# Gated linear attention: level products over the later half-blocks alone, two token tiles to a PSUM bank

## What is computed

```
bcum = jnp.cumsum(gi, axis=2)                                  # log decays, per key channel
diff = bcum[:, :, :, None, :] - bcum[:, :, None, :, :]
decay = jnp.exp(jnp.where(causal, diff, NEG_INF))
attn = jnp.einsum('bhid,bhjd,bhijd->bhij', qi, ki, decay)      # i the query, j the key, j <= i
o_intra = jnp.einsum('bhij,bhje->bhie', attn, vi)
```

## Time and profile before

| | |
|---|---|
| median of 3 runs | 1090.76 us (1087.79 to 1096.67) |
| the profiled execution's own time | 1091.74 us |
| its span, from first to last instruction | 1089.9 us |
| TensorE busy | 1007.9 us, 92% |
| TensorE weight loads busy (beside the products) | 831.4 us, 76% |
| VectorE busy | 446.7 us, 41% |
| ScalarE busy | 442.5 us, 41% |
| GpSimd busy | 191.7 us, 18% |
| mean granted TensorE clock | 0.961 of full speed |

### The profile page before, as it was taken

How to read it: one execution, slowest core, us unless ns; L and a number is a source line. 1 busy time by engine, 2 the same in 40 slices (tenths; PEclk the granted TensorE clock), 3 DMA queues, 4 the chain that set the end, 5 groups by cost and what they waited for, 6 DMA issues and landing times.

```text
span 1089.9 us, 13989 instructions
## 1 busy us (share of the span) xinstructions
PE 1007.9 (92%) x5164; PEld 831.4 (76%) x5164; DVE 446.7 (41%) x826; ACT 442.5 (41%) x757; POOL 191.7 (18%) x176
## 2 busy tenths in 40 slices
PE   1899998999898999999989999399999999899994
PEld 1687766888787878878878888388888888788883
DVE  2214534343214555555666652822323232323335
ACT  1642233242334565656774433523333333322222
POOL 1232222332341333323440000100000000000001
PEclk9999997997999999999999999599999999999998
DMA  5421111341223222226428532022222222212221
GB/s 185 137 77 58 59 39 58 93 156 62 71 86 100 92 93 68 92 97 230 138 78 299 192 119 101 23 75 98 97 97 95 97 96 96 96 62 98 95 72 78
DMA packets 37492, 110.58 MB, mean 101 GB/s; under 512 B 4065, under 2 KB 8161, under 8 KB 36930
## 3 DMA queue, kind: packets, MB, share of 16 engines
q1 hardware_dynamic: 37200, 109.44, 29.8%
q10 hardware_dynamic: 242, 0.47, 0.1%
HBM read 94.16 MB, written 12.58 MB: 98 GB/s over the span
## 4 chain that ended last, share of the span: by engine, by line
PE 88%; DVE 4%; ACT 3%; DMA 2%; issue 2%; POOL 1%; POOLq 0%; DVEq 0%; ACTq 0%
PE bank L1395 25%; PE bank L1396 24%; PE bank L1397 24%; PE bank L1455 3%; PE bank L559 2%; DMA onehot<-distance_onehot 2%; PE bank L551 1%; PE bank L573 1%; PE bank L550 1%; PE bank L571 1%; PE bank L517 1%; PE bank L577 1%; ACT w_hi L786 1%; ACT band L806 1%; DVE x L1281 0%
## 5 line engine op out<-in xcount | busy, mean ns | idle before, releaser
L1395 PE MATMUL bank<-h_hi,w_lo 128*128 128x512 f32 (+1 forms) x712 | 286.4, 402 | 4.8 <-DVE cqs L1126 3.0
L1396 PE MATMUL bank<-h_lo,w_hi 128*128 128x512 f32 (+1 forms) x712 | 281.6, 395 | 0.0
L1397 PE MATMUL bank<-h_hi,w_hi 128*128 128x512 f32 (+1 forms) x712 | 281.0, 395 | 0.0
L786 ACT ACTIVATE w_hi<-w_raw 128x1024 fp32r<-128x1024 f32 (+1 forms) x87 | 91.3, 1051 | 215.2 <-PE bank L1397 214.9
L1395 PEld LDWEIGHTS bank<-h_hi,w_lo 128*128 128x128 f32 (+1 forms) x712 | 136.2, 191 | 39.1 <-issue 12.6
L1397 PEld LDWEIGHTS bank<-h_hi,w_hi 128*128 128x128 f32 (+1 forms) x712 | 135.7, 191 | 29.9
L1396 PEld LDWEIGHTS bank<-h_lo,w_hi 128*128 128x128 f32 (+1 forms) x712 | 136.2, 191 | 26.1
L719 POOL TENSOR_TENSOR w_lo<-w_raw,w_hi 128x1024 fp32r<-128x1024 f32 (+1 forms) x37 | 86.9, 2349 | 209.9 <-ACT w_hi L786 209.9
L972 ACT ACTIVATE w_hi<-w_raw 128x1024 fp32r<-128x1024 f32 x44 | 46.7, 1061 | 157.2 <-PE bank L1397 157.2
L1328 DVE TENSOR_TENSOR w_lo<-w_raw,w_hi 128x1024 fp32r<-128x1024 f32 x44 | 54.0, 1226 | 104.1 <-ACT w_hi L972 104.1
L726 POOL TENSOR_TENSOR sc<-sc,ast 128x512 f32<-128x512 f32 (+1 forms) x96 | 66.2, 721 | 143.8 <-DVE ast L490 109.9
(11 more groups left out here) (257 smaller groups left out, 1531.7 us busy)
## 6 DMA issues: line engine op xcount, KB each, us to landing
w_raw<-wpack SPq DMA_DIRECT2D x147, 512.0 KB, 3.3
gate_logits<-gl_out SPq DMA_DIRECT2D x24, 256.0 KB, 2.2
gl_in<-gate_logits SPq DMA_DIRECT2D x24, 256.0 KB, 3.6
xs<-x_in SPq DMA_DIRECT2D x4, 512.0 KB, 9.3
bias_bands<-band SPq DMA_DIRECT2D x1, 2048.0 KB, 8.3
fullb<-bias_bands SPq DMA_DIRECT2D x16, 128.0 KB, 2.6
ckx<-cks SPq DMA_DIRECT2D x16, 128.0 KB, 2.5
ob<-gla_out SPq DMA_DIRECT2D x2, 1024.0 KB, 6.1
```

What stands on the lines that cost most here:

```text
L786: sa.activation(wh[:, b, 0:n], raw[:, s, 0:n], ACT.Copy).then_inc(w_hi, 1)
L1395: mm(out, ll, rh, start=start, stop=False, skip_group_check=True)
L1396: mm(out, lh, rl, start=False, stop=False, skip_group_check=True)
L1397: return mm(out, lh, rh, start=False, stop=stop, skip_group_check=True)
```

## The change

The seven levels with a half-block get two bank steps in place of four: for each head only the 64 tokens of later halves are streamed, so a head's product is 128 by 64 and two tiles with four heads each fill a bank. The order of the 16 matmuls in a bank step is by array row half, with one `other_rows` in each. VectorE copies a pair of tiles with one `copy_predicated` whose destination and mask are strided to the later halves. The diagonal keeps its form, under new functions `level_own` and `gla_pick_own`. The list `AUX` and the waits that name a level's last tile follow.

```diff
-AUX = (["gates", "z0", "z1", "bT0", "bT1"] + [f"lv{l}_{t}" for l in range(8) for t in range(NT)]
+AUX = (["gates", "z0", "z1", "bT0", "bT1"] + [f"lv{l}_{t}" for l in range(7) for t in range(2)] + [f"lv7_{t}" for t in range(NT)]
...
-                    aux_full(sa, "lv5_3")
+                    aux_full(sa, "lv5_1")
...
-                    aux_full(ve, f"lv{l - 2}_3")
+                    aux_full(ve, f"lv{l - 2}_1")
...
-                for t in range(NT):
+                s = LEVELS[l]
+                for t in range(2):
                     aux_full(ve, f"lv{l}_{t}")
...
                     if l > 0:
                         aux_out(ve, f"lv{l - 1}_{t}")
-                    ve.copy_predicated(attnT[:, t, :, :], lmask[:, l:l + 1, :].broadcast_to([P, 4, P]),
-                                       aux_bank(f"lv{l}_{t}")[:, :].rearrange("p (h c) -> p h c", h=4)
+                    later = attnT[:, 2 * t:2 * t + 2, :, :].rearrange("p t h (n u s) -> p (t h) n u s", u=2, s=s)
+                    below = lmask[:, l, :].rearrange("p (n u s) -> p n u s", u=2, s=s)
+                    ve.copy_predicated(later[:, :, :, 1, :],
+                                       below[:, :, 1, :].unsqueeze(1).broadcast_to([P, 8, 64 // s, s]),
+                                       aux_bank(f"lv{l}_{t}")[:, :].rearrange("p (h n s) -> p h n s", h=8, s=s)
                                        ).then_inc(aux_free[AUX_AT[f"lv{l}_{t}"] % 2], 1)
+            def gla_pick_own():
+                for t in range(NT):
+                    aux_full(ve, f"lv7_{t}")
+                    aux_out(ve, f"lv6_{t // 2}")
+                    ve.copy_predicated(attnT[:, t, :, :], lmask[:, 7:8, :].broadcast_to([P, 4, P]),
+                                       aux_bank(f"lv7_{t}")[:, :].rearrange("p (h c) -> p h c", h=4)
+                                       ).then_inc(aux_free[AUX_AT[f"lv7_{t}"] % 2], 1)
...
             def level(l):
+                s = LEVELS[l]
+                for pair in range(2):
+                    name = f"lv{l}_{pair}"
+                    aux_free_for(name)
+                    te.wait_ge(z_ready, 2 * l + 2)
+                    for odd in range(2):
+                        if odd:
+                            other_rows(last)
+                        for t in range(2):
+                            for p in range(2):
+                                both = zz[64 * odd:64 * odd + 64, l % 2, 512 * p + P * (2 * pair + t):512 * p + P * (2 * pair + t) + P]
+                                at_ = 256 * t + 64 * (2 * p + odd)
+                                last = mm(aux_bank(name)[:, at_:at_ + 64], both,
+                                          both.rearrange("p (n u s) -> p n u s", u=2, s=s)[:, :, 1, :], start=True, stop=True)
+                    last.then_inc(aux_done, 1)
+            def level_own():
                 for t in range(NT):
-                    name = f"lv{l}_{t}"
+                    name = f"lv7_{t}"
...
-                if 6 <= c < 14:
+                if 6 <= c < 13:
                     level(c - 6)
+                if c == 13:
+                    level_own()
```

More of the change, by code:

```diff
@@ L1163, in _ @@
                                      b3[:, :, P - 1:P].broadcast_to([P, 8, P]), b3, ALU.subtract).then_inc(e_ready, 1)
-                    gla_pick(7)
+                    gla_pick_own()
                     ve.wait_ge(ex_ready, 10)
@@ L1442, in level @@
             def level(l):
+                s = LEVELS[l]
[14 more added lines that the diff above has]
+            def level_own():
                 for t in range(NT):
-                    name = f"lv{l}_{t}"
+                    name = f"lv7_{t}"
                     aux_free_for(name)
-                    if l < 7:
-                        te.wait_ge(z_ready, 2 * l + 2)
                     for h in (0, 2, 1, 3):
@@ L1452, in level @@
                         cols = slice(512 * p + P * t, 512 * p + P * t + P)
-                        kk = zz[b:b + 64, l % 2, cols] if l < 7 else gk[b:b + 64, cols]
-                        qq = zz[b:b + 64, l % 2, cols] if l < 7 else gq[b:b + 64, cols]
-                        last = mm(aux_bank(name)[:, P * h:P * h + P], kk, qq, start=True, stop=True)
+                        last = mm(aux_bank(name)[:, P * h:P * h + P], gk[b:b + 64, cols], gq[b:b + 64, cols],
+                                  start=True, stop=True)
                     last.then_inc(aux_done, 1)
```

## The result

The changed kernel takes 1101.29 us (median of 20 runs, 1095.86 to 1108.30), the kernel before 1091.28 (20 runs, 1087.63 to 1096.67). The ratio is 1.0096, with a 95% interval of 1.0076 to 1.0116. The forecast was 1083 us, with a range of 1077 to 1091. The profiled executions are 11.6 us apart in span (1101.5 against 1089.9).

A forecast was written before the change was run, and what follows sets the result against it. TensorE, busy 92% of the span, was taken to bound the kernel. Level stages shrink from 4.57 to 3.44 us, saving 6.8 to 7.9 us in seven; from the 1090.76 median this gave 1083 us, range 1077 to 1091.

The forecast's parts named there:

- granted clock 1.00 in all seven: Sign of the forecast case: TensorE's clock stays at full speed through all seven edited level stages; that case had 67%.
- rival A: Clock falls in the thinner level stages, 3.4 us lost per fall; a fall in each of seven gives 1107 us; 12%.
- Moving columns halved: Level products: record spacing follows the weight columns, staying 0.11 us, so halved streaming buys nothing between records.
- Rival C: Level products: record spacing follows the moving columns after all, saving 2.26 us a level, 15.8 us: 1075 us; 7%.
- The tail: At two row waits and the hand-over to the projection: shorter last record (218 ns, not 272) saves 0.054 us each.
- steps one and three: First and last eight one-sided loads of a level stage: 1.21 and 1.08 us before taking off the shorter tail.
- Step two: Middle of a level stage, eight odd beside eight even loads: halves overlap, added loads 0.059 us each, 1.31 us.
- Rival B: Middle step: the second pair does not overlap the first, a stage takes 4.3 us, saving only 2 us: 1089; 12%.
- Waits: In a level stage: four row waits become two and the one bank wait goes, as two banks hold the level.
- VectorE's copies: 14 of 28 copies go, 11 us beside TensorE, worth nothing directly; strided copy taken at 0.79 us, bound at twice that.
- rival D: The strided copy is so dear, 2.6 us against 0.79, that VectorE binds: a little over 1091 us; 2%.
- What else must be ready: Weight split, ScalarE's `gv` copies and exponential, and DMA issues are in time, so the shorter stages meet no new wait.

The follow-up runs named there:

- run 2: Changed kernel with its order kept, but each product streams all 128 columns again (scores not the reference's): 1087.94 us, ratio 0.9955.
- run 3: Changed kernel with the 64 moving columns taken contiguous, as the first 64 tokens, in place of the strided later ones: 1100.69 us, ratio 1.0067.
- run 8: Changed kernel with 96 moving columns on average (odd heads 128, even 64) and the two row halves by turns in the middle step: 1082.96 us, ratio 0.9923.
- run 6: Kernel before, all 128 columns and four tiles, each level cut into five pieces inside the next projection chunk: 1092.12 us, ratio 1.0018.
- run 7: Changed kernel with odd heads first and streaming 128 columns, even heads 64, so 96 on average: 1094.75 us, ratio 1.0033.
- run 10: Repeat of run 8 (changed kernel with 96 columns on average and row halves by turns): 1085.73 us, ratio 0.9940.
- run 1: Kernel before with only the moving columns halved to 64 and copies narrowed likewise, old order kept: 1101.71 us, ratio 1.0095.
- run 9: Changed kernel with 64 moving columns, its only edit being row halves by turns in the middle of a level: 1092.89 us, ratio 1.0007.
- run 4: Changed kernel with each level's products cut at the row waits into three pieces inside the next projection chunk: 1089.49 us, ratio 0.9975.
- run 5: Run 4's kernel with the middle piece's two row halves issued by turns, one odd, one even: 1086.30 us, ratio 0.9959.

## Why the prediction was wrong

**The step that failed** is "granted clock 1.00 in all seven": rival A was given 12% and decided all. What the prediction held against it was that the `w1k` chunk, with 66 columns to 0.057 us, kept the clock at 1.00 for 3.64 us. I took its share of streaming time, about half, as the same thing. It did not carry over. The chunk uses 128 rows in one stretch of 3.6 us, the level stages 64 rows in seven stretches; which difference counts stays open, since no run varied it. The clock had also fallen behind the neighbouring `w1v` chunk, so one stretch that holds was weak evidence for seven that repeat. The row that should have weighed more is the earlier trace rows: a stream bound by its weight loads, in which the columns do not fill the interval, fell within 3 us of its start with no idle time in it. The price of a fall was set at 3.4 us, that of a fall of 6.8 us; only four of the seven were so long, and the mean price is 2.5. The chances of this rival do not fit together either: three falls or more got 6%, and the six or more that a loss of over 1% needs got 7%.

The Trainium skill, in "TensorE: Matmul & The Clock Gate", section "Why this matters for your kernels", warns of idle gaps between bursts of matmuls. No such gap explains these falls: the longest idle time of a stage's load engine was 0.35 us, in the stages at which the clock fell and in those of before alike. What differs between run 2, with no fall, and the changed kernel, with seven, is the columns streamed at the same number of loads.

**Moving columns halved: spacing.** Right. One-sided loads are (0.96 - 0.19) / 7 = 0.11 us apart with 64 columns as with 128. Rival C is out.

**The tail.** Right in size: the load engine idles 0.20 us at a row wait in place of 0.25, and steps one and three measure as forecast. The record itself does not show it: its median is 272 ns after as before, not the 218 that the prediction took; only the waits got shorter. Weight loads of a stage at full clock after, answering to the earlier trace rows:

```profile
101.69 0.96 PEld L1469 LDWEIGHTS bank<-zz 64*128 64x128 f32 x8 [0.35 <-issue]
102.85 1.46 PEld L1469 LDWEIGHTS bank<-zz 64*128 64x128 f32 x16 [0.20 <-PE bank L1469]
104.51 0.96 PEld L1469 LDWEIGHTS bank<-zz 64*128 64x128 f32 x8 [0.20 <-PE bank L1469]
105.55 0.29 PEld L1408 LDWEIGHTS bank<-w_hi,h_lo 128*128 128x128 f32 x1
```

Step one 102.85 - 101.69 = 1.16 (forecast 1.21 - 0.05), step three 1.04 (1.08 - 0.05).

**Step two was mis-sized:** 104.51 - 102.85 = 1.66 us against 1.31 - 0.05 = 1.26. The added eight loads were priced at 0.059 each, as if the halves overlapped all along; they overlap only from the sixth load on. Rival B is true in part: 0.4 of its 0.8 us. With turns the step is 114.02 - 112.82 = 1.20, and the stage 3.40, the 3.44 of the forecast. Had the clock held, the change as written would have saved 7 x 0.71 = 5.0 us and not 7.9, about 1086 us: the forecast of 1083 would have missed by 3.

**Waits.** The bank wait is gone and four row waits are two, as said.

**VectorE's copies.** Right for five levels of seven: the strided copy takes 0.70 to 0.74 us there, against the 0.79 taken. At half-blocks 2 and 1 all four copies take 1.31 us, inside the bound of twice 0.79 but not foreseen: the products of the earlier trace rows showed no such step. Runs 2 and 3, which leave the copies alone, have the same step (1.31 to 1.32 us). TensorE never waits for them, so it costs nothing here, and rival D (2.6 us a copy) is out. Line 1090, all seven levels, duration ns as in the earlier trace rows, then copies of half-blocks 4 and 2:

```profile
L1090 DVE COPY_PREDICATED attnT<-lmask,bank x14: 701/732/1315, 91.3 to 164.9; 128x512 f32<-128x512 uint16 x14
```

```profile
138.84 0.71 DVE L1090 COPY_PREDICATED attnT<-lmask,bank 128x512 f32<-128x512 uint16 x1 [6.36 <-PE bank L1469]
...
151.53 1.31 DVE L1090 COPY_PREDICATED attnT<-lmask,bank 128x512 f32<-128x512 uint16 x1 [7.27 <-PE bank L1469]
```

**What else must be ready.** Right: TensorE is busy throughout every chunk behind a stage.

## What to carry to other kernels

Before thinning a stretch of matmuls, ask what sets their interval. If it is the weight load, fewer moving columns buy little time (0.21 us of 4.07 a stage here), and the granted clock may fall, as it did at every stage here; what follows is unedited dense work at half speed, the dearest place to lose. It can be worth streaming columns that nobody reads (run 8). Where products use half of the rows, issue the two halves by turns.

## What the runs showed of the hardware

- Falls of the granted clock from 1.00 to 0.50 in or right behind the seven level stages, in one profiled execution of each kernel: with 128 columns a record, none (before, run 2; in run 6 one, behind 1.8 us of idle time); with 96, four (run 7), and none or one where the halves go by turns (runs 8, 10); with 64, six or seven (after, runs 1, 3, 9), with or without stride, turns or the old order; with 64 between dense products, none (runs 4, 5).
- TensorE lets the two row halves run side by side, but with eight records of one in front it started the other only after five (run 7). By turns, 16 loads take 0.97 us (run 9) and not 1.46.
- A change between 64-row and 128-row products costs a little more than the row wait that it can cover: 9.71 us interleaved against 9.54 (run 4).
- A `copy_predicated` of 128x512 float32 from PSUM takes 0.70 to 0.74 us with its destination and mask strided in runs of 64 down to 4 elements, and 1.31 us in runs of 2 and 1.
